# Reordering the operators, and the way of the state-space input, in an FFN / S5 / attention trunk

## The reference, cut to what matters

```
x = x + 0.5 * swiglu(rms_norm(x, g[0]), w_in, w_out)     # d_ff 2816
h = rms_norm(x, g[1])
# s5_mixer(h): 64 groups of 16 channels, 64 complex states each
#   state_t = lam_bar * state_(t-1) + b_bar u_t
#   y_t = Re(C state_t) + D u_t ; y = gelu(y) ; z = y @ w_glu
x = x + z[:1024] * sigmoid(z[1024:])
x = x + 0.5 * swiglu(rms_norm(x, g[2]), ...)
# then keys and values, layer 1 with attention, final rms_norm
```

## Time and profile before

| | |
|---|---|
| median of 3 runs | 1887.57 us (1883.63 to 1888.64) |
| profiled execution | 1892.09 us, its span 1890.3 us |
| busy | PE 1829.4 (97%), DVE 949.2 (50%), ACT 604.0 (32%), POOL 292.6 (15%) |
| mean granted clock of PE | 0.978 of full speed |
| last FFN product before the state-space stage | PE free at 425.93 us |
| first GLU product | 524.73 us |

### The profile page before, as it was taken

The page is one execution under the profiler, slowest core; times in us unless marked ns, Lnnn a source line. Parts: engine busy times, 40 slices in busy tenths (PEclk is TensorE's granted clock), DMA queues, the critical chain, the costliest instruction groups (busy, mean ns, idle before and its releaser), DMA issues.

```text
span 1890.3 us, 21606 instructions
## 1 busy us (share of the span) xinstructions
PE 1829.4 (97%) x8188; PEld 1488.1 (79%) x8188; DVE 949.2 (50%) x1177; ACT 604.0 (32%) x808; POOL 292.6 (15%) x260
## 2 busy tenths in 40 slices
PE   8988999996999999999999999999989999999997
PEld 6867788874878888888888888888766778888886
DVE  7687857634644543443346434433486353443333
ACT  6322223320133432332234333322325343333221
POOL 7955534001301400000000000000100100000000
PEclk9988999996999999999999999999989999999999
DMA  5344544457643233223223222233310223323321
GB/s 189 112 122 134 162 141 138 152 194 222 188 130 101 90 99 100 90 98 101 91 98 94 96 100 96 92 101 99 119 56 1 78 89 100 99 90 100 100 90 45
DMA packets 80481, 207.83 MB, mean 110 GB/s; under 512 B 24688, under 2 KB 35056, under 8 KB 78368
## 3 DMA queue, kind: packets, MB, share of 16 engines
q1 hardware_dynamic: 76016, 186.19, 31.1%
q0 software_dynamic: 3104, 18.55, 2.9%
q10 hardware_dynamic: 1296, 2.20, 0.3%
HBM read 183.84 MB, written 23.07 MB: 109 GB/s over the span
## 4 chain that ended last, share of the span: by engine, by line
PE 88%; DVE 4%; POOL 3%; DMA 2%; ACT 1%; issue 1%; SPq 1%; DVEq 0%; ACTq 0%
PE bank L1455 26%; PE bank L1457 26%; PE bank L1456 26%; PE bank L1778 1%; PE bank L1631 1%; PE bank L1780 1%; PE bank L1797 1%; PE bank L1529 1%; PE bank L1655 1%; PE bank L1662 1%; POOL b_pow L544 1%; POOL b_pow L541 1%; PE bank L1640 1%; DMA s_u<-h_norm 1%; POOL s_tmp L542 1%
## 5 line engine op out<-in xcount | busy, mean ns | idle before, releaser
L1030 DVE TENSOR_TENSOR w_split<-w_raw,w_split 128x1024 fp32r<-128x1024 f32 x299 | 394.2, 1322 | 650.3 <-ACT w_split L685 649.6
L1455 PE MATMUL bank<-h_split,w_split 128*128 128x512 f32 x1512 | 592.7, 392 | 6.1 <-DVE w_split L1030 3.8
L1457 PE MATMUL bank<-h_split,w_split 128*128 128x512 f32 x1512 | 589.1, 390 | 0.0
L1456 PE MATMUL bank<-h_split,w_split 128*128 128x512 f32 x1512 | 588.9, 390 | 0.0
L685 ACT ACTIVATE w_split<-w_raw 128x1024 fp32r<-128x1024 f32 x299 | 315.7, 1059 | 686.2 <-PE bank L1457 678.5
L1455 PEld LDWEIGHTS bank<-h_split,w_split 128*128 128x128 f32 x1512 | 284.3, 188 | 67.9 <-issue 4.0
L1455 PE MATMUL bank<-g_split,w_split 128*128 128x512 f32 (+1 forms) x854 | 331.3, 388 | 2.0 <-DVE g_split L1256 2.0
L1456 PEld LDWEIGHTS bank<-h_split,w_split 128*128 128x128 f32 x1512 | 284.5, 188 | 59.7 <-issue 1.2
L1457 PEld LDWEIGHTS bank<-h_split,w_split 128*128 128x128 f32 x1512 | 284.4, 188 | 59.2
L1456 PE MATMUL bank<-g_split,w_split 128*128 128x512 f32 (+1 forms) x854 | 328.1, 384 | 0.0
L1457 PE MATMUL bank<-g_split,w_split 128*128 128x512 f32 (+1 forms) x854 | 328.1, 384 | 0.0
(11 more groups left out here) (265 smaller groups left out, 1216.2 us busy)
## 6 DMA issues: line engine op xcount, KB each, us to landing
w_raw<-wstream SPq DMA_DIRECT2D x299, 512.0 KB, 3.5
op_slots<-s_ops POOLq DMA_DIRECT2D x5, 2048.0 KB, 12.3
s_ops<-ops_out SPq DMA_DIRECT2D x8, 1024.0 KB, 4.0
op_slots<-s_ops SPq DMA_DIRECT2D x3, 2048.0 KB, 7.9
s_ops<-c_pow POOLq DMA_DIRECT2D x8, 512.0 KB, 4.3
s_ops<-k_window SPq DMA_DIRECT2D x64, 64.0 KB, 3.4
x_res<-xT SPq DMA_DIRECT2D x8, 256.0 KB, 7.8
bc_in<-bcd POOLq DMA_DIRECT2D x8, 256.0 KB, 5.2
```

Of the source, the lines that this page charges most:

```text
L1030: tt(W[:, r, 1, :], RAW[:, r, :], W[:, r, 0, :].bitcast(F32), ALU.subtract).then_inc(s_lo, 1)
L1455: mm(bank, hi, x_hi, start=start, stop=True, skip_group_check=True)
L1456: mm(bank, hi, x_lo, start=False, stop=True, skip_group_check=True)
L1457: return mm(bank, lo, x_hi, start=False, stop=True, skip_group_check=True)
```

## The change

1. `make_powers(1)` runs before the `PA` tables; `BC` has two buffers and is fetched one block ahead; `b_bar` has places of its own (`B_BAR_AT`), the tables others; the tables are stored apart (`store_tables`).
2. In the output stage of `FFN0A2` ACT (`s5_input`) squares each finished tile, multiplies x by its gain into step order, stores it, and loads it back (`load_u`) one tile later, without normalising it. POOL sums the squares of tiles 0 to 6 (`sum_squares`); PE multiplies by ones twice, after the last tile. SP loads u for tiles 6 and 7. The layout in DRAM is `[tile, step, channel, group, time]`, so one DMA serves a tile; the channels of the weights are permuted on the host to suit.
3. The root is taken on 64 columns (`RT`: PE's sums times the mask `C_T8`, then a reduction over each eight tokens), and u is multiplied by it after loading: tile 0 by DVE, the others by POOL (`scale_u`). A partition of the loaded u belongs to one step offset and one channel, so it needs one token in eight; the mask picks it.
4. The swaps of halves are two copies of 64 partitions on ACT in place of a product on PE. PE's order in the loop is changed; so are ACT's, DVE's and POOL's.
5. Six operator slots at other places: 0 is loaded when H is free, 1 and 2 as before, 3 to 7 by SP. y goes back block by block.
6. `keep_warm`: 2 and 1 dummies about the sum, 4 behind it, in place of 11.

```diff
-TABLES_AT = {(FFN0A1, IN, 6): 0, (FFN0A1, IN, 8): 1, (FFN0A1, OUT, 1): 2, (FFN0A1, OUT, 4): 3, (FFN0A2, IN, 1): 4,
-             (FFN0A2, IN, 4): 5, (FFN0A2, IN, 7): 6, (FFN0A2, IN, 10): 7}
+B_BAR_AT = {(FFN0A1, IN, 1): 0, (FFN0A1, IN, 5): 1, (FFN0A1, IN, 7): 2, (FFN0A1, IN, 10): 3, (FFN0A1, OUT, 2): 4,
+            (FFN0A1, OUT, 5): 5, (FFN0A2, IN, 3): 6, (FFN0A2, IN, 6): 7}
+TABLES_AT = {(FFN0A1, IN, 9): 0, (FFN0A1, OUT, 1): 1, (FFN0A1, OUT, 4): 2, (FFN0A2, IN, 1): 3, (FFN0A2, IN, 4): 4,
+             (FFN0A2, IN, 6): 5, (FFN0A2, IN, 8): 6, (FFN0A2, IN, 10): 7}
...
+SUMS = {N_S5: (0, 0), N_IN0B: (8, 6), N_KV: (16, 13), N_DQ: (24, 20), N_IN1B: (32, 27), N_FINAL: (40, 34)}
+SQ_OF, ADD_OF = ({n: v[q] for n, v in SUMS.items()} for q in range(2))
+ADDED = {n: ADD_OF[n] + (DT - 2 if n in (N_S5, N_FINAL) else DT - 1) for n in SUMS}
...
+    SLOT = [at(f"op_slot{i}", [P, OPS], F32, o) for i, o in enumerate(
+        (o_h, o_g + 48 * K, o_g + 64 * K, o_g, o_g + 16 * K, o_g + 32 * K))]
+    N_SLOTS = len(SLOT)
...
+            def store_tables(k):
+                sp.wait_ge(s_phase, 2 * k + 2)
+                sp.dma_start(ops_dram[k][:, O_COS:O_C], OUTB[:, O_COS:O_C]).then_inc(s_tabst, 16)
...
+            sp.wait_ge(s_used, FFN0A2 + 3 * HALF)
+            sp.dma_start(op_slot(3), ops_dram[3]).then_inc(s_slot[3], 16)
+            for k in range(DT - 2, DT):
+                sp.wait_ge(s_ust[k], 16)
+                sp.dma_start(UY[:, k * GB:(k + 1) * GB, :], u_dram[k].rearrange("t c g j -> (t c) g j")
+                             ).then_inc(s_uld[k], 16)
+            for k in (4, 5):
+                sp.dma_start(op_slot(k), ops_dram[k]).then_inc(s_slot[k], 16)
+            for k in (6, 7):
                 sp.wait_ge(s_yp, k - N_SLOTS + 1)
-                sp.dma_start(op_slot(k), ops_dram[k]).then_inc(s_again[k - N_SLOTS], 16)
-            for q in range(QUARTERS):
-                sp.wait_ge(s_y, BLOCKS // QUARTERS * (q + 1))
-                for t in range(T):
-                    sp.dma_start(y_dram[q * QD:(q + 1) * QD, t, :].rearrange("(g c) j -> c g j", c=GC),
-                                 UY[t * GC:(t + 1) * GC, q * QG:(q + 1) * QG, :]).then_inc(s_yst[q], 16)
-                sp.wait_ge(s_yst[q], 16 * T)
-                for k in range(q * QK, (q + 1) * QK):
-                    sp.dma_start(YT[:, k, :], y_dram[k * P:(k + 1) * P].rearrange("p t j -> p (t j)")
-                                 ).then_inc(s_yld[q], 16)
+                sp.dma_start(op_slot(k), ops_dram[k]).then_inc(s_slot[k], 16)
+            sp.wait_ge(s_yp, 3)
...
+                if k + 1 < BLOCKS:
+                    pool.dma_start(BC[(k + 1) % 2][:], bcd[k + 1]).then_inc(s_bc[(k + 1) % 2], 16)
+                bc = BC[k % 2]
+                pool.wait_ge(s_bc[k % 2], 16 * (k // 2 + 1))
...
             powers(tt, link, PB, 7, t1, t2)
+            make_powers(1)
             squared(tt, link, (PA[:, 0, 1, :], PA[:, 1, 1, :]), (PB[:, 0, 4, :], PB[:, 1, 4, :]), t1, t2)
             powers(tt, link, PA, 7, t1, t2)
             nc.gpsimd.memset(TM[:, 0:8], 0.0).then_inc(s_near, 1)
             pool.wait_ge(s_near, 1)
-            for k in range(1, BLOCKS):
+            for k in range(2, BLOCKS):
...
+            for k in (1, 2):
                 pool.dma_start(op_slot(k), ops_dram[k]).then_inc(s_slot[k], 16)
+            pool.wait_ge(s_used, FFN0A2 + 2 * HALF)
+            pool.dma_start(op_slot(0), ops_dram[0]).then_inc(s_slot[0], 16)
+            sum_squares(N_S5, DT - 1)
+            def scale_u(k):
+                pool.wait_ge(s_uld[k], 16)
+                uk = UY[:, k * GB:(k + 1) * GB, :]
+                tt(uk, uk, RT[:].unsqueeze(1).broadcast_to([P, GB, STEPS]), ALU.mult).then_inc(s_un, 1)
...
+            pool.wait_ge(s_rstd, N_S5 + 1)
+            scale_u(1)
+            scale_u(2)
+            input_cos(0)
+            scale_u(3)
+            input_cos(1)
+            for k in range(BLOCKS):
+                state_cos(k)
+                if k + 2 < BLOCKS:
+                    input_cos(k + 2)
+                if k + 4 < BLOCKS:
+                    scale_u(k + 4)
...
+            def s5_input(k):
+                act.wait_ge(s_x, X_BASE[FFN0A2] + k + 1)
+                if k == 0:
+                    act.wait_ge(s_opdma, 16 * OPS_STORES * BLOCKS)
+                    act.wait_ge(s_tabst, 16 * BLOCKS)
+                square(N_S5, k)
+                if k >= N_RING:
+                    act.wait_ge(s_ust[k - N_RING], 16)
+                xk = X[:, k, :].rearrange("p (j t) -> p t j", t=T)[:, ::-1, :]
+                nc.scalar.activation(HN[:, k % N_RING], xk, ACT.Identity, scale=col(G_S5 + k)).then_inc(s_hn, 1)
+                act.wait_ge(s_hn, k + 1)
+                act.dma_start(u_dram[k].rearrange("t c g j -> (c g) t j"), HN[:, k % N_RING]).then_inc(s_ust[k], 16)
+                if 1 <= k < DT - 1:
+                    load_u(k - 1)
+            def load_u(k):
+                act.wait_ge(s_ust[k], 16)
+                act.dma_start(UY[:, k * GB:(k + 1) * GB, :], u_dram[k].rearrange("t c g j -> (t c) g j")
+                              ).then_inc(s_uld[k], 16)
...
-            root(N_S5)
-            for k in range(DT):
-                act.wait_ge(s_hn, k + 1)
-                act.dma_start(u_dram[k * P:(k + 1) * P], HN[:, k]).then_inc(s_ust[k // QK], 16)
+            root(N_S5, RT)
+            nc.scalar.preload_act_table(ACT.Gelu_apprx_tanh)
...
+            def swap_halves(dst, src):
+                nc.scalar.activation(dst[0:64, :], src[64:P, :], ACT.Copy)
+                return nc.scalar.activation(dst[64:P, :], src[0:64, :], ACT.Copy)
...
             for k in range(3):
                 copy_s(k)
+                swap_input(k)
+            swap_state(0)
             for k in range(BLOCKS):
+                if k + 1 < BLOCKS:
+                    swap_state(k + 1)
+                gelu(k)
                 if k + 3 < BLOCKS:
                     copy_s(k + 3)
-                gelu(k)
-            for k in range(DT):
-                act.wait_ge(s_yld[k // QK], 16 * QK)
-                nc.scalar.activation(G[:, k, 0, :], YT[:, k, :], ACT.Copy).then_inc(s_y_hi, 1)
+                    swap_input(k + 3)
+                elif k < BLOCKS - 1:
+                    y_hi(2 * (k - 5))
+                    y_hi(2 * (k - 5) + 1)
...
-            mean_rcp(N_S5, BK[BASE[FFN0A2]])
+            dve.wait_ge(s_opdma, 16 * OPS_STORES * BLOCKS)
+            dve.wait_ge(s_tabst, 16 * BLOCKS)
+            dve.wait_ge(s_cpst, 16 * BLOCKS)
+            nc.vector.memset(XS[:, :, :, 0:1], 0.0).then_inc(s_zero, 1)
+            dve.wait_ge(s_ssq, N_S5 + 1)
+            ut = UT[:].rearrange("p (j t) -> p j t", t=T)
+            link(tt(ut, BK[BASE[FFN0A2]][:].rearrange("p (j t) -> p j t", t=T),
+                    COLS[:, C_T8:C_T8 + T].unsqueeze(1).broadcast_to([P, STEPS, T]), ALU.mult))
+            link(nc.vector.reduce_sum(RT[:], ut, AX.X))
+            link(ts(RT[:], RT[:], 1.0 / D, EPS, ALU.mult, ALU.add))
+            nc.vector.reciprocal(RT[:], RT[:]).then_inc(s_rcp, 1)
             dve.wait_ge(s_rstd, N_S5 + 1)
-            for k in range(DT):
-                stt(HN[:, k].rearrange("p t j -> p j t"), X[:, k, :].rearrange("p (j t) -> p j t", t=T),
-                    col(G_S5 + k), RSTD[:].rearrange("p (j t) -> p j t", t=T), ALU.mult, ALU.mult).then_inc(s_hn, 1)
-            nc.vector.memset(XS[:, :, :, 0:1], 0.0).then_inc(s_zero, 1)
+            dve.wait_ge(s_uld[0], 16)
+            tt(UY[:, 0:GB, :], UY[:, 0:GB, :], RT[:].unsqueeze(1).broadcast_to([P, GB, STEPS]), ALU.mult).then_inc(s_un0, 1)
...
+            scan(0)
+            scan(1)
+            for k in range(BLOCKS):
+                turn_state(k)
+                if k + 2 < BLOCKS:
+                    scan(k + 2)
...
-            def stats_behind(n, stage):
-                def between(d):
-                    if d >= 2:
-                        wide_stat(n, stage, d - 2)
-                return between
-            ffn_out(FFN0A2, stats_behind(N_S5, FFN0A2))
-            for k in range(DT - 2, DT):
-                wide_stat(N_S5, FFN0A2, k)
+            ffn_out(FFN0A2)
+            total = BK[BASE[FFN0A2]]
+            keep_warm(2, RSTD, BK[1])
+            pe.wait_ge(s_sum, ADDED[N_S5])
+            mm(total[:], ONES[:], ACC[:], start=True, stop=True, skip_group_check=True)
+            keep_warm(1, RSTD, BK[1])
+            pe.wait_ge(s_sq, SQ_OF[N_S5] + DT)
+            mm(total[:], ONES[:], SQ[:, (DT - 1) % 2, :], start=False, stop=True, skip_group_check=True).then_inc(s_ssq, 1)
...
-            pe.wait_ge(s_hn, 1)
-            keep_warm(11, RSTD, BK[7])
-            pe.wait_ge(s_jp, 16)
+            keep_warm(4, RSTD, BK[7])
             pe.wait_ge(s_zero, 1)
             step_input(0)
-            swap_input(0)
             step_input(1)
-            for k in range(BLOCKS + 1):
-                if k + 1 < BLOCKS:
-                    swap_input(k + 1)
```

(40 more changed lines are left out.)

196 lines of the change are left out of this document (90 added, 106 removed).

## The result

| | before | after |
|---|---|---|
| median of the runs | 1887.57 us (1881.61 to 1891.15, 5 runs) | 1873.33 us (1872.39 to 1873.49, 5 runs) |
| span of the profiled execution | 1890.3 us | 1871.5 us |
| GLU begins | 524.73 us | 506.38 us |

The ratio is 0.9929, 95% interval 0.9908 to 0.995: faster by 0.7%, some 14 us, where 42.5 us were forecast. Three of these five runs of the kernel before took over 1886 us, as only 8 of 31 later ones did; against the medians of those, 1883.0 to 1883.8 us, the change is worth some 10 us. The time lies outside the range, 28 us above the forecast. The direction was right, and so was the mechanism that was to decide the size (the clock stays at 1.2 GHz in the block loop); four other terms were not.

The account below looks back on a forecast made before the run. TensorE was taken as the bound (88% of the chain that ended last). Savings of 24.5 (operators), 4.4 (sum of squares) and 13.6 us (state-space stage), 42.5 together, from the median 1887.6 gave 1845 us, range 1836 to 1854.

Parts of the forecast that it names:

- Part 2: Output stage: five `wide_stat` products leave PE's path, saving 4.4 us; ACT's new waits in `load_u` cost nothing.
- rival (d): Output stage: ACT stands in `load_u` for late stores, splits come late, PE stands at each tile; slower, 1940 us, chance 0.03.
- a sign of being wrong: Output stage: the prediction listed PE waiting for `w_split` there among the observations that would show it wrong.
- 14 us of slack: Output stage: weight splits run three packs ahead of PE, so ACT's waits up to about 14 us cost nothing.
- Part 3: Last FFN product to first step input: only u's scale is missing, step input at 434.0, clock still 2.4 GHz.
- Rival (b): Before the first step input: scale late, dummies run out, clock falls already, all groups at 1.2 GHz; 1851 us, chance 0.09.
- Part 1: Operator blocks, first FFN half: PE's waits for `b_pow` and the slow clock behind them go, saving 24.5 us.
- 1 us to spare: Operator block 2: `b_pow` ready at 128 or 129, PE wants it at 129.6; the tightest place.
- rival (c): Operator blocks: POOL still late at block 2 (and 4), a wait up to 5 us, slow block behind; 1851 us, chance 0.09.
- Part 4: State-space stage, before the first `from_states`: PE stands about 3.0 us, bounds 2.4 to about 5 us.
- Part 5: Block loop to the GLU: clock stays at 1.2 GHz, 19 groups take 64.4 us, GLU begins 14.5 us earlier.
- rival (a): Block loop: PE stays at or returns to 2.4 GHz, saving 76 us in all; 1811 us, chance 0.10.

Follow-up runs that it names:

- operators alone: The kernel before with only the operator part of the change (POOL's order, `BC` in two buffers, `b_bar` and table places, tables stored apart): 1868.33 us, ratio 0.991.
- state-first order: The changed kernel with each block's `scan` followed at once by its `turn_state` on DVE, so `turn_state(0)` stands ahead of `scan(1)`: 1869.7 us, ratio 0.9917.
- the two other edits: Loads of u three tiles behind their stores and `b_bar` of block 1 a tile earlier; with wide products in pause and loop, on the changed kernel: 1833.8 us.

## Why the prediction was wrong, by its own steps

Spans of the profiled executions fell by 18.8 us where 42.5 were counted, 23.7 short. By stretches, forecast and measured in the time of the changed kernel:

| stretch | forecast | measured | short by |
|---|---|---|---|
| up to the last FFN product | 397.0 (425.93 - 24.5 - 4.4) | 405.6 | 8.6 |
| to the first step input | 8.1 | 19.3 | 11.2 |
| to `from_states(0)` | 11.8 | 15.7 | 3.9 |
| to the GLU | 64.4 | 65.8 | 1.4 |
| from the GLU on | 1366.5 (1365.6 + 0.9) | 1365.1 | -1.4 |

Another 4.6 us come from the base: the forecast took the difference over to the median, but the kernel before was profiled 4.5 us above its median and the changed one exactly at it.

**Part 2, on ACT's waits in `load_u`, "I take nothing"**, is the step that failed. It was also the first event of rival (d), and a wait for `w_split` in the output stage was a sign of being wrong: both came, at a small size. The wait was priced by when it would stop PE through late splits, with 14 us of slack, and against that bound it was almost harmless: 2.2 us of PE for 13.7 us of ACT, so the slack was some 11.5 us and not 14. But ACT's squares feed the sum that ends the stage, and that chain has no slack at the end: each us that ACT is late there is a us of PE. Moving the loads away gave 11.3 us. The landing was also off: 9.0 us was the row beside three operator loads, and it was 19.3 here. The two cases differ in the queue of the loads and in the pieces of the store, 256 bytes now, which the prediction named and gave no price; beside loads they moved one to a packet of the loads. The removal of the five `wide_stat` products was right: last FFN product at 406.52 with operators alone and 402.34 with the new sum and the loads moved, 4.2 us against 4.4.

**Part 3, step input 8.1 us behind**, assumed that PE's dummies ran straight into the sum. From the last statistics product on it was right: 420.46 to 424.86 is 4.4 us, counted 4.6. All that was missing lay ahead of it, 9.53 us of wait and the clock at 1.2 GHz behind it (0.50 from 417 to 420 us). Rival (b) had the clock fall before the first step input. It did, by Part 2's cause and not by late scales, but wide products (the sum and its dummies) had it back at 1.00 from 421 us on, so the first groups did not run slowly and the rival as priced did not occur.

**Part 1, block 2 "1 us to spare"** (rival (c)). It was the right place to name and too kindly taken: 4.24 us of POOL's wait for `b_bar` of block 1 and 0.96 for block 2 were not counted. The price was a wait of 2.67 us and 3.4 us at 1.2 GHz (0.58 over 4 us), 1.7 us lost. Of the rest of the 8.6 us, 2.2 are `w_split` at 383.70, 0.4 a later start (block 0 at 69.49 instead of 69.13) and 0.6 a wait on `g_split` at 155.30; some 1 us has no one place. An earlier `b_bar` of block 1 took 1.8 us off the whole. The two large waits went as forecast, 19.4 us in profiled executions; in medians the part is worth 15.2.

**Part 4, a pause of 3.0 us**, was 6.58. ACT had the swapped state at 435.5 us, 10.7 us behind the first step input where 10.1 were counted, but DVE was in `scan(1)` until 438.6, and DVE, not ACT, was the limit. The sum had put DVE's products at their undisturbed length of the earlier trace rows; beside POOL the scans took 2.5 and 3.5 us instead of 1.57. The state-first order showed it: 3.56 us.

**Part 5** was right in mechanism and number: 19 groups, 65.8 us against 64.4, clock 0.50, and 17.7 us back with wide products in the loop. One reading behind it was too strong: it said that the clock returned only when two swaps followed each other at 474.40, but two did so at 464.11 and 465.97 as well, and it stayed at 0.50. The forecast did not hang on that. The Trainium skill's rule (TensorE: Matmul & The Clock Gate, Part 1, "What's actually happening"), that activity releases the throttle, was too coarse for this: a PE busy for 65.16 of 65.9 us with 64-column products stayed at 1.2 GHz. So rival (a) was no outcome of this change. Its clock can be had, though: with wide products put back, and the two other edits, the kernel is 39.5 us faster.

## What to carry to other kernels

Price a new wait on a helper engine against every chain that runs through it, not only the one with slack: here the weight splits had some 11 us of it and the sum of squares none, and the lag between two engines that took turns at nearly PE's pace was not made up in six tiles. Before moving wide products off a TensorE whose remaining work is narrow, look at the clock: they may be what holds it at 2.4 GHz, and a few products of zeros (here 13) can be worth more than the work saved. And take the base of a forecast from an execution as long as the profiled one, or say by how much they differ.

## What the runs showed of the hardware

- Groups of 64 columns did not raise the clock in 65.9 us of almost unbroken work, and kept it for 12 us after a filled pause. Two products of 512 columns in a row were followed by 1.00 in two places (449.55 us with wide products in the loop, 474.40 in the kernel before) and not in a third (464.11 in the kernel before).
- A store of 256 KB in 256-byte pieces landed in 2.7 us without the operator loads and in 9.5 to 22.4 us when issued while three loads of 2048 KB from another engine's queue were under way; from 366 to 370 us that queue moved 106 packets with 1.47 MB and the store's 105 with 0.03 MB. ScalarE was also held 3.54 to 4.46 us in the issue of a third store, with two under way.
- Eight scans of 64 columns on VectorE took 1.57 us with GpSimd idle and 2.51 to 3.54 us beside its products; a 128x512 product of VectorE took 1.15 us instead of 0.69.
